# Two-layer hybrid backbone on one core: 128-slot blocks of the first layer's larger experts done full width, in three one-pass products of split weights and rows

## The reference

```python
def run_block(args):
    xb, e = args
    return (jax.nn.silu(xb @ w1[e]) * (xb @ w3[e])) @ w2[e]
```

## Time and profile before

| what | us |
|---|---|
| median of three runs | 2400.26 (2398.15 to 2403.87) |
| profiled execution, its own time | 2387.92 |
| its span, first to last instruction | 2386.1 |
| layer 0's experts, first w2 load issued to last down's end | 748.1 to 1346.6 |
| layer 1's experts, the same | 1808.4 to 2337.4 |
| busy in the span: TensorE, VectorE, ScalarE, GpSimd | 2203.8, 778.7, 639.9, 182.4 |

### The profile page before, as it was taken

One profiled execution on the slowest core, in us unless ns is written; L12 is line 12 of the kernel. 1 busy time (PEld: TensorE's weight loads), 2 busy tenths in 40 slices (PEclk: granted clock), 3 DMA queues, 4 the chain that ended last, 5 costly groups with the idle time before them and its releaser, 6 DMA issues. The chain is left out here.

```text
span 2386.1 us, 36238 instructions
## 1 busy us (share of the span) xinstructions
PE 2203.8 (92%) x15702; PEld 1103.2 (46%) x15702; DVE 778.7 (33%) x1296; ACT 639.9 (27%) x1041; POOL 182.4 (8%) x126
## 2 busy tenths in 40 slices
PE   7999989989987999999999889998988999998884
PEld 5888875536752333333333345444853333332222
DVE  7333336655252111111111263766552111111105
ACT  5411015553141111111111255655231111111112
POOL 0010000000000000000000212451000000000003
PEclk9999999999999999999999999999999999999986
DMA  9201026037459898999999431001139999999996
GB/s 357 58 27 36 27 111 250 1 106 263 126 184 381 355 417 344 384 374 414 414 412 413 162 110 35 27 18 36 36 136 367 423 415 412 421 428 426 427 426 232
DMA packets 147809, 595.93 MB, mean 250 GB/s; under 512 B 25444, under 2 KB 62016, under 8 KB 122944
## 3 DMA queue, kind: packets, MB, share of 16 engines
q1 hardware_dynamic: 117536, 515.42, 54.1%
q0 software_dynamic: 11952, 43.52, 4.8%
q10 hardware_dynamic: 18160, 34.62, 4.0%
HBM read 534.81 MB, written 58.72 MB: 249 GB/s over the span
## 5 line engine op out<-in xcount | busy, mean ns | idle before, releaser
L1949 PE MATMUL ph<-w,x_t 128*32 128x512 f32 x6016 | 677.6, 603 | 30.5 <-DMA w<-in_exp_w 28.2
L1949 PEld LDWEIGHTS ph<-w,x_t 128*32 128x32 f32 x6016 | 190.8, 111 | 439.2 <-issue 417.0
L1962 PE MATMUL py<-w,g_t 128*32 128x512 f32 x3008 | 342.9, 596 | 6.5 <-DMA w<-in_exp_w 5.5
L2063 DVE TENSOR_TENSOR hidden<-hidden,ph 64x512 f32<-64x512 f32 x94 | 102.2, 1087 | 736.8 <-ACT hidden L2021 736.8
L2021 ACT ACTIVATE hidden<-ph 64x512 f32<-64x512 f32 x94 | 55.5, 591 | 682.3 <-PE ph L1949 682.3
L1962 PEld LDWEIGHTS py<-w,g_t 128*32 128x32 f32 x3008 | 95.1, 110 | 211.3 <-issue 210.0
L2297 PE MATMUL z<-hT,w_cd 128*128 128x512 f32 (+1 forms) x448 | 184.5, 569 | 0.0
L1566 POOL DMA_INDIRECT x_rows<-h_tokens,index x47 | 44.3, 943 | 1713.6 <-PE px L1934 975.2
L768 PE MATMUL z<-h_high,w_hi 128*128 128x512 f32 (+1 forms) x432 | 160.2, 371 | 3.2 <-DVE h_low L863 2.9
L769 PE MATMUL z<-h_low,w_hi 128*128 128x512 f32 (+1 forms) x432 | 155.7, 360 | 0.0
L770 PE MATMUL z<-h_high,w_lo 128*128 128x512 f32 (+1 forms) x432 | 155.4, 360 | 0.0
(11 more groups left out here) (348 smaller groups left out, 2372.9 us busy)
## 6 DMA issues: line engine op xcount, KB each, us to landing
w<-in_exp_w SPq DMA_DIRECT2D x192, 2048.0 KB, 19.6
ada_raw<-in_ada_w SPq DMA_DIRECT2D x13, 2048.0 KB, 9.1
y_slots<-y_rows ACTq DMA_DIRECT2D x188, 128.0 KB, 9.0
w<-in_ada_w SPq DMA_DIRECT2D x8, 2048.0 KB, 13.9
y_slots<-zero SPq DMA_DIRECT2D x29, 512.0 KB, 15.3
h_tokens<-h_rows ACTq DMA_DIRECT2D x18, 512.0 KB, 5.4
w_ab<-in_w_in_ab SPq DMA_DIRECT2D x14, 512.0 KB, 3.8
ada_first<-in_ada_w SPq DMA_DIRECT2D x3, 2048.0 KB, 17.0
```

Of the source, the lines that this page charges most:

```text
L1949: ins = pe.matmul(ph[row:row + UNIT, :], xt[:, k, at:at + UNIT], w13[place[2 * b + n] % RING][:, half, k, :], start=(k == 0), stop=(k == K ...
L1962: ins = pe.matmul(py[b % 2][row:row + UNIT, :], gt[:, k, n * UNIT:(n + 1) * UNIT], w2[place[2 * b + n] % RING][:, k, half * 512:(half + 1) ...
L2063: dve.tensor_tensor(hid[PAIR:P, :].rearrange("s (k q) -> s q k", k=FT), hid[0:PAIR, :].rearrange("s (q k) -> s q k", k=FT), ph[PAIR:P, :]. ...
```

## The change

In layer 0 only, a quad whose four units belong to one expert becomes one item of 128 slots; all others stay two pairs. The order of the ranks is laid out anew so that each expert of 4, 5 or 6 units has such a quad: 13 of the 26. The quads then come in turn, one full, one of two pairs.

A full item goes by 12 chunks, 8 of w1 and w3 side by side and 4 of w2, each 128 x 1024. ScalarE copies the chunk to one of four buffers w_high (F32R). VectorE subtracts it from the weights and writes the low part in the weights' own place. TensorE does six products of 128 x 128 by 128 x 512 for each chunk. The rows (x_high, x_low) and the activated rows (g_split) are split in the same way. silu, product and the copies out take 128 rows at a time.

w_high and x_high (later g_split) lie where the first four of eight slices of xT are. SP therefore saves these (2.6 MB) at the end of layer 0's merge, and loads them back behind the last weights.

```diff
+def block_order(room):
+    of = {n: [r for r in range(NE) if room[r] == n] for n in range(1, 7)}
+    heavy = [(of[2].pop(), r) for r in of[6]] + [(of[3].pop(), r) for r in of[5]]
+    light = [(of[3].pop(), r) for r in of[1]]
+    while of[2]:
+        light.append((of[2].pop(), of[2].pop()))
+    order = []
+    for n, r in enumerate(of[4]):
+        order += [r, *heavy.pop(0)]
+        if n == len(of[4]) // 2:
+            order += heavy.pop(0)
+        order += light.pop(0)
...
@@ merge, SP
+                    sp.wait_ge(s_x, HALF * NC)
+                    sp.dma_start(self.xs[:, 0:HALF, :], self.xT[:, 0:HALF, :]).then_inc(s_kept, 16)
+                    sp.wait_ge(s_kept, 16)
...
@@ experts, SP (i counts items: full ones and pairs)
                     if j >= RING:
-                        sp.wait_ge(s_a, last[j - RING] // 2 + 1)
+                        sp.wait_ge(s_a, last[j - RING] + 1)
...
+                if FULL[layer]:
+                    sp.wait_ge(s_b, max(chunk_at) + 1)
+                    sp.dma_start(self.xT[:, 0:KT // 2, :], self.xs[:, 0:KT // 2, :]).then_inc(s_back, 16)
...
@@ experts, TensorE
+                def split_products(c, x_hi, x_lo, lows, outs, first, end):
+                    highs = [self.w_high[:, c % HI_RING, half * 512:(half + 1) * 512] for half in range(2)]
+                    pe.wait_ge(s_hi, c + 1)
+                    for half in range(2):
+                        pe.matmul(outs[half], x_hi, highs[half], start=first, stop=False)
+                    for half in range(2):
+                        ins = pe.matmul(outs[half], x_lo, highs[half], start=False, stop=False)
+                    ins.then_inc(s_wf, 1)
+                    pe.wait_ge(s_lo, c + 1)
+                    for half in range(2):
+                        ins = pe.matmul(outs[half], x_hi, lows[half], start=False, stop=end)
...
@@ experts, ScalarE
+                def high(i, ks):
+                    j = place[items[i][1]]
+                    for k in ks:
+                        c = chunk_at[i] + k
+                        if c >= HI_RING:
+                            act.wait_ge(s_wf, c - HI_RING + 1)
+                            act.wait_ge(s_lo, c - HI_RING + 1)
...
+                for i in range(-1, N):
+                    if i >= 0 and full[i]:
+                        g_high(i)
+                        high(i, range(KT, KT + FT))
+                    if i + 1 < N:
+                        if full[i + 1]:
+                            high(i + 1, range(HI_RING, KT))
+                        silu(i + 1)
+                        if ends_quad[i + 1] and items[i + 1][0] + 1 < NQUAD:
+                            x_out(items[i + 1][0] + 1)
+                    if i + 2 < N and full[i + 2]:
+                        high(i + 2, range(0, HI_RING))
+                    if i >= 0:
+                        y_out(i)
...
@@ experts, VectorE
+                for i in range(-1, N):
+                    if i + 1 < N and full[i + 1]:
+                        x_low(i + 1)
+                        low(i + 1, range(0, HI_RING))
+                    if i >= 0:
+                        g_out(i)
+                        if full[i]:
+                            low(i, range(KT, KT + FT))
+                    if i + 1 < N:
+                        if full[i + 1]:
+                            low(i + 1, range(HI_RING, KT))
+                        product(i + 1)
```

More of the change, by code:

```diff
@@ L1623, in _ @@
                 sp.wait_ge(s_table, 1)
-                first = self.expert_of(sp, 0)
+                first = self.expert_of(sp, layer, 0)
                 sp.wait_ge(s_te, 2 * nt)
@@ L1851, in experts @@
         NU = len(place)
-        NPAIR, NQUAD = NU // 2, NU // 4
-        last = {j: u for u, j in enumerate(place)}
+        NQUAD = NU // 4
+        items = work_items(layer)
+        N = len(items)
+        full = [n == 4 for q, u, n in items]
+        chunk_at = {i: 12 * b for b, i in enumerate(i for i in range(N) if full[i])}
+        last = {place[u + k]: i for i, (q, u, n) in enumerate(items) for k in range(n)}
+        ends_quad = [i + 1 == N or items[i + 1][0] != items[i][0] for i in range(N)]
+        bufs, done_before, copies = [], [], [0]
+        filled = [0, 0]
+        for i in range(N):
+            at = copies[i] % 2
+            bufs.append((at, 1 - at) if full[i] else (at,))
+            done_before.append(tuple(filled))
+            for u in bufs[i]:
+                filled[u] += 16 if full[i] else 32
+            copies.append(copies[i] + len(bufs[i]))
         with ExitStack() as ctx:
@@ L1856, in experts @@
             xr, s_x = ring["x_rows"], ring["s_x"]
+            if FULL[layer]:
+                with ExitStack() as same_place:
+                    xt_low = self.sb(same_place, "x_low", [P, KT, P], F32R)
             xt = self.sb(ctx, "x_t", [P, KT, P])
@@ new lines, in up_full @@
+                def up_full(i):
+                    q, u, _ = items[i]
+                    pe.wait_ge(s_xt, q + 1)
+                    pe.wait_ge(s_xl, list(chunk_at).index(i) + 1)
+                    for k in range(KT):
+                        ins = split_products(chunk_at[i] + k, self.x_high[:, k, :], xt_low[:, k, :],
+                                             [ring["w13_low"][place[u] % RING][:, half, k, :] for half in range(2)],
+                                             (ph[:], ph3[:]), k == 0, k == KT - 1)
+                    ins.then_inc(s_a, 1)
@@ L1967, in _, with down @@
+                def down(i):
+                    pe.wait_ge(s_gte, i + 1)
+                    if copies[i + 1] > 2:
+                        pe.wait_ge(s_ye, copies[i + 1] - 2)
+                    (down_full if full[i] else down_pair)(i)
                 transpose_x(0)
                 up(0)
-                for b in range(NPAIR):
-                    pe.wait_ge(s_g, b + 1)
+                if ends_quad[0]:
+                    transpose_x(1)
+                for i in range(N):
+                    pe.wait_ge(s_g, i + 1)
@@ L2033, in _ @@
                 x_out(0)
[L2034 to L2040, removed]
+                if full[0]:
+                    high(0, range(0, HI_RING))
+                for i in range(-1, N):
[6 more added lines that the diff above has]
+                        silu(i + 1)
+                        if ends_quad[i + 1] and items[i + 1][0] + 1 < NQUAD:
+                            x_out(items[i + 1][0] + 1)
[3 more added lines that the diff above has]
+                        y_out(i)
@@ L2060, in _, with x_low @@
             def _(dve):
[L2061 to L2071, removed]
+                def x_low(i):
+                    dve.wait_ge(s_xt, items[i][0] + 1)
+                    dve.tensor_tensor(xt_low[:], px[:].rearrange("p (k c) -> p k c", k=KT), self.x_high[:].bitcast(F32),
+                                      ALU.subtract).then_inc(s_xl, 1)
```

205 lines of the change are left out of this document (154 added, 51 removed).

## The result

The changed kernel takes 2346.28 us (median of 4 runs, 2345.29 to 2350.35) against 2400.02 (2398.15 to 2403.87): a ratio of 0.9777, with a 95% interval of 0.976 to 0.9794. That is 53.7 us less; 48.5 were forecast, 2351.8 us, with a range of 2334 to 2376. The profiled execution took 2345.69 us with a span of 2343.8.

A forecast was written before the change was run, and what follows sets the result against it. TensorE was taken to bound layer 0's expert stage, with transfers the nearer limit after the change: 540 + 8 + 2 us make a stage of 550, 48.5 less, so 2400.3 - 48.5 = 2351.8 us, range 2334 to 2376.

The forecast's parts named there:

- What bound the kernel before: Layer 0's expert stage: TensorE sets the pace, 26 quads in sequence at 22.81 us each, 593.1 us.
- Part 1: Full blocks on TensorE: 17.9 us each against 22.81, saving 4.9 us 13 times, 64 us.
- The ends: TensorE's time at the stage's ends beside its blocks: 5.4 us, of 1.5, 2.5, 0.9 and 0.5.
- Part 2: ScalarE's and VectorE's added work in full blocks: covered with 1.4 us to spare, costed at nothing.
- Rival (b): Hand-offs bind in full blocks: low parts take 1.7 us, stage 566 us, time 2368 us; chance 0.15.
- Part 3: Layer 0's stage: transfers at 420 GB/s become the nearer limit, 83.2 us per five experts against TensorE's 81.4; 548 us.
- rival (a): Layer 0's stage: transfers keep up, TensorE alone sets the pace; stage 534.5 us, time 2336 us; chance 0.12.
- Rival (c): Layer 0's stage: transfers can give no more than 375 GB/s, nothing is won, 2400 us; chance 0.04.
- The start: Start of layer 0's stage: expert 1's weights come late, 3.1 us of the 8 us counted there.
- Part 4: TensorE's clock in layer 0's stage: halved for a time after waits for weights, 2 us lost.
- Rival (d): TensorE's full blocks: half of the products at half clock, 26.0 us a block, 2442 us; chance 0.03.
- Part 5: Saving xT after layer 0's merge and loading it back behind the last w2: covered, costed at nothing.

The follow-up runs named there:

- (2): The changed kernel with its new order and save of xT, but every quad as two pairs; 2393.2 us, stage 597.1 us.
- (3): The changed kernel with its 13 full blocks in plain float32, without high and low parts; 2394.5 us, stage 595.8 us.
- Experiment 8: The changed kernel with a further VectorE operation over 512 columns ahead of each low part; 2366.3 us, stage 569.4 us.
- experiment 5: The changed kernel without the product low rows x high weights in the full blocks; 2333.6 us, stage 539.5 us.
- experiment 7: The changed kernel with a further VectorE operation over 128 columns ahead of each low part; 2341.1 us, stage 549.0 us.

## Why the prediction was right, and where it was off

**What bound the kernel before** (TensorE at 22.81 us a quad): shown. Full blocks shorten the stage and the order alone does not (2). Seven of them shorten TensorE's busy time by 27 us (593.1 to 566.3), thirteen by 54 (to 538.7).

**Part 1, 17.9 us a block:** 18.25 measured. The product distance of 0.2264 from layer 0's projection held, 1.357 us a chunk; an up takes 0.2 us more than its eight chunks, and the down came to 5.68 instead of 5.4. A full block and the two pairs after it take 41.23 where the sum had 40.7. The ends were too dear, 5.4: before its first up the stage has 2.8 us and not 4, since the 1.5 as now already hold a wait for the copied rows, and the 2.4 for x_low come in its place. By the rows of the changed kernel the ends are the waits of 2.4 (x_low), 1.0 (hidden) and 0.5 (g_t), less 0.7 by which the first rows' turn lies ahead of the stage: 3.3. TensorE's own path was therefore 13 x 41.23 + 3.3 = 539.3, not 534.5. That the split, not the width, brings it (3) was not argued in the prediction, only implied by the price.

**Part 2, nothing for ScalarE and VectorE:** right. The forecast worked out 1.4 us to spare in a block, up to the end of the up. By that measure it was 2.6 (1011.0 to 1013.6), and 2.1 up to the last two products, which are what waits for the last low part. Operations at distances of 1.14 instead of durations of 1.23 are about 0.7 of the difference, shorter waits (0.34 and 0.51, where 1.1 was counted) 0.25, and TensorE's side was 0.2 longer. Two terms were mis-sized and cancel: the full item's product took 0.69 us and not 1.09, its silu 1.07 and not 0.6. Rival (b), 2368, needed low parts of 1.7 us; they stayed at 1.22 beside transfers at 425 GB/s. Experiment 8 made such a kernel: 1.74 us a low part with the added operation, a stage of 569.4 us where (b) had 566.

**Part 3, the transfers set the pace:** this is the step that failed in its size, and with it the order of the two limits. 420 GB/s was taken from 520 us of layer 1's stage. The changed kernel's stage moves 425 from 800 to 1250 us, and experiment 5's 426 over 520 us, so a group of five experts needs 82.2 us, not 83.2. (A part of this is the stretch chosen: the changed kernel moves 421 over its middle 520 us, and layer 1's stage 422 over its middle 450.) TensorE's group is 2 x 41.23 = 82.5, not 81.4. The two are equal within 0.3 us, so there were 3.8 us of waits for weights where 10 to 20 were forecast, and TensorE is, by a hair, still what ends last. That the time came out right within 5.5 us is in part luck: the forecast let the wrong one of the two limits set the pace, and its errors of 1% in the two, in opposite directions, move a stage with nearly equal limits by little. Of rival (a), "transfers keep up", the mechanism was nearly the truth; its time, 2336, left out the 4.8 us of part 1, the 3.8 of waits and the slower clock behind them. Rival (c), that 375 GB/s was all this stage's transfers could give, fell. The Trainium skill, "DMA: Bandwidth & Descriptors", section "Where 436 GB/s comes from", has the HBM side bind at about 358 GB/s; for one core running alone as here the trace disagrees, with experiment 5's 426.

**The start,** 3.1 us for the second expert's weights: 1.8 were waited. **Part 4:** one up of 8.69 us behind the wait of 1.8, at a granted clock of 0.81: 1.6 us lost. The wait of 1.73 at 1033.6 cost no clock, its up took 7.07. Rival (d) fell: the clock was 0.99 over the stage. The first block of all started at the lower level too, 1.2 GHz (granted clock 0.50 from 752.4 to 755.1): TensorE had idled 1.7 us before the rows' turn and 2.4 after it. Its first products on TensorE's timeline:

```profile
752.43 1.19 PE L2040 MATMUL ph<-w_high,x_high 128*128 128x512 f32 x2 [2.42 <-DVE x_low L2232]
...
755.12 0.85 PE L2040 MATMUL ph<-w_high,x_high 128*128 128x512 f32 x2
...
756.73 0.62 PE L2040 MATMUL ph<-w_high,x_high 128*128 128x512 f32 x2
```

The first chunk takes 2.69 us, the second 1.61, where the up at 1002.58 takes 1.48 and 1.38: 1.4 us lost. So the clock cost 3.0 us in all, where part 4 counted 2. 539.3 + 3.8 + 1.6 + 1.4 = 546.1, and the stage took 546.4.

**Part 5, nothing for xT:** right, both transfers landed where nothing waited for them, though they took 11.8 and 10.4 us and not 6.

## What to carry to other kernels

Price a change by the distance of starts of the same instruction in the same kernel, and price the next limit in the same unit (here us for five experts). When the two come out within a few per cent, the gain ends there, and only something that shortens both is worth doing next. A float32 product costs nearly four one-pass ones (products of type F32R; 0.858 against 0.226 us for 512 columns), so three products of split operands took 0.68 us in place of 0.86. They paid here because ScalarE had 1.05 us and VectorE 1.14 us for each chunk to spare, and because the weights may be overwritten. When an experiment gives the expected number, look in its timeline whether it came about as expected: experiment 7's did not. Compare kernels by the stage that the change touches when the rest of the execution scatters by more than the effect.

## What the runs showed of the hardware

- Transfers held 426 GB/s over 520 us beside 252 us of VectorE's and 241 us of ScalarE's work on the same memory, and VectorE's operations became no slower (1.226 us for 1024 columns in the projection, with 32 GB/s from 100 to 300 us, and 1.220 here).
- VectorE's operations of one kind in a row start closer than their duration: 1.14 against 1.22 us; an added one of 0.69 costs 0.60, and one of 0.29 costs 0.20.
- silu over 128x512 took 1.07 us in the full items and 0.59 over 64x512 in the pairs; the product took 0.69 over 128x512 and 1.09 over 64x512. In each case the longer one is the one that writes hidden in another order; no run tells this apart from the number of rows.
- Parts of the kernel that no edit touched took between 460.6 and 470.9 us from execution to execution, while layer 1's expert stage, unchanged too, took 528.3 to 529.7 in twelve profiles, and layer 0's of the kernel before 597.6 and 598.5 in two.
